# One-core decoder layer, routing stage reordered: turns of the second block between the first block's router products, residual products moved into later waits

## What is computed

```
x = x + mix @ w_out
h = rmsnorm(x, ln_ffn_g)
logits = h @ w_router + b_router            # 256 x 32
top_val, top_idx = top_k(logits, 4); probs = softmax(top_val)
# for each expert e, on the tokens that chose it:
a = clamped_swiglu(xb @ w_gate[e] + b_gate[e], xb @ w_up[e] + b_up[e])
y = a @ w_down[e] + b_down[e]
x = x + (sum over the chosen experts of prob * y)
out = rmsnorm(x, ln_final_g)
```

## Time and profile before

| | us |
|---|---|
| median of 3 runs | 1135.55 |
| lowest, highest | 1134.89, 1136.51 |
| the profiled execution | 1135.38 |
| its span | 1133.3 |
| TensorE busy | 1094.9 (97%) |
| VectorE busy | 315.9 (28%) |
| ScalarE busy | 205.5 (18%) |
| read from HBM | 437.69 MB, 387 GB/s over the span |

### The profile page before, as it was taken

How to read it: one execution, slowest core, us unless ns; L and a number is a source line. 1 busy time by engine, 2 the same in 40 slices (tenths; PEclk the granted TensorE clock), 3 DMA queues, 4 the chain that set the end, 5 groups by cost and what they waited for, 6 DMA issues and landing times.

```text
span 1133.3 us, 12456 instructions
## 1 busy us (share of the span) xinstructions
PE 1094.9 (97%) x5393; PEld 499.3 (44%) x5393; DVE 315.9 (28%) x684; ACT 205.5 (18%) x367; POOL 19.7 (2%) x27
## 2 busy tenths in 40 slices
PE   8999999999999999999999999999999999999997
PEld 6888888733343333333333333333333333333332
DVE  7566778421111111111211111111111111111121
ACT  6445547210000000001100000000000000000011
POOL 1000110000000000000000000000000000000000
PEclk9999999999999999999999999999999999999999
DMA  9754229999999999999999999999999999999996
GB/s 360 263 177 158 110 77 404 412 396 412 426 435 428 434 426 430 434 426 429 433 431 428 430 432 428 430 430 432 429 432 430 431 430 433 432 431 430 433 422 258
DMA packets 38439, 439.23 MB, mean 388 GB/s; under 512 B 3050, under 2 KB 4610, under 8 KB 19844
## 3 DMA queue, kind: packets, MB, share of 16 engines
q1 hardware_dynamic: 38100, 438.41, 92.2%
q10 hardware_dynamic: 304, 0.33, 0.1%
HBM read 437.69 MB, written 1.05 MB: 387 GB/s over the span
## 4 chain that ended last, share of the span: by engine, by line
PE 72%; DMA 25%; DVE 1%; issue 1%; ACT 0%; DVEq 0%; POOLq 0%; POOL 0%; ACTq 0%
PE ps L1153 42%; DMA pair<-in_w_up_dram 25%; PE ps L778 5%; PE ps L1177 5%; PE ps L1082 3%; PE ps L880 2%; PE ps L808 2%; PE ps L816 2%; PE ps L933 1%; PE ps L1130 1%; PE ps L935 1%; PE ps L934 1%; PE ps L1021 1%; PE ps L1023 1%; PE ps L1022 1%
## 5 line engine op out<-in xcount | busy, mean ns | idle before, releaser
L1153 PE MATMUL ps<-pair,o_t 128*64 128x512 f32 x3072 | 680.6, 595 | 23.2 <-DMA pair<-in_w_gate_dram 19.3
L1153 PEld LDWEIGHTS ps<-pair,o_t 128*64 128x64 f32 x3072 | 217.0, 137 | 442.6 <-issue 411.5
L1627 DVE TENSOR_SCALAR work<-ps 128x512 f32<-128x512 f32 x32 | 22.1, 692 | 494.9 <-PE ps L1153 494.9
L712 ACT ACTIVATE o_t<-ps 128x512 f32<-128x512 f32 x32 | 19.1, 597 | 297.9 <-PE ps L778 297.9
L1177 PE MATMUL ps<-attn,o_t 64*128 64x512 f32 x256 | 71.5, 639 | 0.0
L699 ACT ACTIVATE attn<-work 128x512 f32<-128x512 f32 x32 | 20.1, 629 | 261.2 <-DVE work L1627 261.2
L1082 PE MATMUL ps<-xs,work 128*64 128x512 f32 x256 | 61.0, 593 | 0.0
L778 PEld LDWEIGHTS ps<-cst,work 128*128 128x128 f32 (+1 forms) x294 | 35.8, 170 | 54.7 <-issue 52.1
L718 ACT ACTIVATE attn<-ps 128x512 f32<-128x512 f32 x31 | 18.5, 598 | 228.0 <-PE ps L1153 228.0
L778 PE MATMUL ps<-cst,work 128*128 128x128 f32 (+1 forms) x294 | 53.0, 296 | 1.0 <-DVE work L1444 0.6
L1633 DVE TENSOR_SCALAR a_rows<-ps 128x512 f32<-128x512 f32 x32 | 22.1, 692 | 103.1 <-PE ps L1153 103.1
(11 more groups left out here) (188 smaller groups left out, 845.6 us busy)
## 6 DMA issues: line engine op xcount, KB each, us to landing
pair<-in_w_gate_dram SPq DMA_DIRECT2D x27, 4096.0 KB, 38.6
pair<-in_w_up_dram SPq DMA_DIRECT2D x26, 4096.0 KB, 36.9
pair<-in_w_down_dram SPq DMA_DIRECT2D x25, 4096.0 KB, 38.3
pair<-in_w_up_dram SPq DMA_DIRECT2D x10, 2048.0 KB, 13.9
pair<-in_w_down_dram SPq DMA_DIRECT2D x9, 2048.0 KB, 14.9
pair<-in_w_gate_dram SPq DMA_DIRECT2D x8, 2048.0 KB, 13.3
wd<-in_w_in_dram SPq DMA_DIRECT2D x5, 2048.0 KB, 9.1
wu<-in_w_in_dram SPq DMA_DIRECT2D x4, 2048.0 KB, 10.8
```

The costliest lines, as they stand in the source:

```text
L1153: mm = pe.matmul(ps[SLOTS * h:SLOTS * h + SLOTS, bank, :], lhs[:, k, :], ring[(at + j) % RING][:, r, 512 * h:512 * h + 512], start=(k == 0 ...
```

## The change

Four edits, three of them on TensorE and one on ScalarE.

- The two calls `turn_residual(1, ...)`, which stood behind both calls of logits of block 0, now stand ahead of each of them. They get waits of their own, since they write banks that may still be read: (1,0) waits for VectorE's copy of (0,0), (1,1) for ScalarE's copy of (0,1).
- On ScalarE the turned copy of (1,0) changes places with the square of (1,1).
- The residual product of (0,0) moves from between the turns and the logits of block 1 to behind the first gather, where that of (0,1) stood. That of (0,1) is cut into two halves of 256 columns, which take the places of two pairs of fillers.
- The position product of block 0, which stood between the two calls of logits of block 1, now stands behind both.

```diff
@@ scalar
             square_residual(1, 0)
+            turned_residual(1, 0)
             square_residual(1, 1)
-            turned_residual(1, 0)
             turned_residual(1, 1)
@@ tensor
             def turn_residual(b, h):
                 pe.wait_ge(res_ready, 2 * b + h + 1)
+                if b and h:
+                    pe.wait_ge(ht_act, 1)
+                elif b:
+                    pe.wait_ge(ht_dve, 1)
@@
-            def residual_in(b, h, start=False):
+            def residual_in(b, h, cut=slice(0, 512), start=False):
-                pe.matmul(ps[:, Y + 2 * b + h, :], ident, xs[:, b, 512 * h:512 * h + 512], start=start, stop=False,
+                pe.matmul(ps[:, Y + 2 * b + h, cut], ident, xs[:, b, 512 * h:512 * h + 512][:, cut], start=start, stop=False,
                           skip_group_check=True)
@@
             pe.wait_ge(bias_lo_ready, 1)
+            turn_residual(1, 0)
             logits_of(0, 0)
+            turn_residual(1, 1)
             logits_of(0, 1)
-            turn_residual(1, 0)
-            turn_residual(1, 1)
-            residual_in(0, 0, start=True)
             logits_of(1, 0)
+            logits_of(1, 1)
             pe.wait_ge(chosen_ready, 1)
             pe.matmul(ps[:, DN, 0:E], tri_far, chosen[:, 0, :], start=True, stop=True).then_inc(pos0_done, 1)
-            logits_of(1, 1)
@@
             gather_block(0)
-            residual_in(0, 1, start=True)
+            residual_in(0, 0, start=True)
             pe.wait_ge(chosen_ready, 2)
             pe.matmul(ps[:, G, E:2 * E], tri_far, chosen[:, 1, :], start=False, stop=True).then_inc(pos_done, 1)
-            keep_busy(2)
+            residual_in(0, 1, cut=slice(0, 256), start=True)
@@
             mm.then_inc(count_done, 1)
-            keep_busy(2)
+            residual_in(0, 1, cut=slice(256, 512))
             turn_gathered(0)
```

## The result

The changed kernel is slower by a little: median 1137.51 us of 22 runs (1136.41 to 1138.34) against 1135.49 us of 22 runs of the kernel before (1134.88 to 1136.51), ratio 1.0017 with a 95% interval of 1.0011 to 1.0023. That is +2.0 us where I had forecast -0.2, and above the range's upper end of 1136.7. The profiled execution took 1136.60, span 1134.6; it lies 0.9 under the changed kernel's own median, so it probably shows a milder case of what the others have. Its routing stage begins 0.41 us earlier, counted from the start of the span (212.55 against 212.96), so places in this stage are compared after adding 0.41 to those of the changed kernel.

A forecast was written before the change was run, and what follows sets the result against it. Bound by the last expert's weights: a first product 0.15 to 0.37 us earlier gives back 0.2 of 0.99 us idle DMA; 1135.38 - 0.2 + 0.17 (median over profiled run) = 1135.35, forecast 1135.3 us, range 1134.3 to 1136.7.

The forecast's parts named there:

- What bounds the kernel: Whole kernel: the last expert's weights set the end; TensorE time counts only through 0.99 us of idle DMA at 225-228 us.
- Turns between logits: Routing stage, from 212.96 us: alternating block 1's turns with block 0's logits completes block 0's logits 1.02 us later.
- VectorE becomes what is late: Before the first gather: it waits for VectorE instead of TensorE's queue, starting at 218.42 instead of 218.79, gain 0.37 us.
- The residual product taken from there: At 215.69 us, ahead of block 1's logits: 0.96 us of TensorE work goes, those logits follow at once, issued by 217.38.
- The first gather to the second position product: Routing stage: gather plus one residual product still take 1.97 us, so the second position product starts at 220.4 to 220.5.
- The halves: Half residual products of 0.43 to 0.51 us in the fillers' places cost nothing; uncovered, each at most 0.2 us.
- The clock rival: Routing stage to first product: four fillers gone and two uncovered waits lower TensorE's clock, costing 3 to 6 us; chance 0.03.
- rivals: Transfers hide all, 1135.55, chance 0.2; block 0 late, 1135.9, 0.12; hole closes further, 1134.6, 0.05; clock lost, 1138-1142, 0.03.

The follow-up runs named there:

- the kernel without fillers: Kernel before without its five fillers behind the position product, the counts and the turned rows, down-bias products split over two experts: 1135.68 us, ratio 0.9999.
- the kernel with the turns alone: Changed kernel with the residual products and all fillers back in their old places: 1135.90 us, ratio 1.0003.
- without the second fall: Changed kernel with the down-bias products of block 1 moved from behind expert 3 to behind expert 4: 1136.43 us, ratio 1.0010.
- with four fillers: Changed kernel with four filler products between the logits of block 0 and those of block 1: 1135.96 us, ratio 1.0002.
- with both cures: Changed kernel with four filler products between the logits of blocks 0 and 1 and the down-bias products split over experts 3 and 4: 1136.19 us, ratio 1.0002.
- the kernel with the late product: Kernel before with five more fillers ahead of the turn of the gathered rows, delaying the first expert product: 1137.87 us, ratio 1.0015.

## Why the prediction was wrong, point by point

- **What bounds the kernel: right.** The end follows the weights. An added 1.06 us at the first product gave +1.0 at the end.
- **Turns between logits: right.** choose(0) was forecast at 215.94 and came at 215.45 + 0.41 = 215.86; its sum at 217.46, and it was 216.97 + 0.41 = 217.38.
- **VectorE becomes what is late: right.** The first gather was forecast at 218.42; it came at 217.84 + 0.41 = 218.25, with an idle stretch that VectorE ended. The gain of 0.37 us up to there was 0.54.
- **The residual product taken from there: this is the step that failed.** I wrote what TensorE no longer does and which queue profits, and gave the engine's clock as a constant. With the product gone TensorE ran nothing but narrow matmuls from 212.55 to 217.84; the clock fell, and the next 1.97 us of work took 3.56. +1.59 against the gain of 0.54 makes the first product 1.0 us later: 12.71 us behind the start of the stage (212.55 to 225.26) instead of 11.70.
- **The first gather to the second position product "is the same work in the new order": right as work, wrong as time.** For the same reason.
- **The halves: right.** The gather that follows the first waited for VectorE, not for them.
- **The clock rival had the right effect and the wrong cause.** It had 0.03. It tied the fall to four fillers gone and to waits of 0.1 and 0.3 us, and I set against it an idle stretch of 0.73 us at full clock. That argument was sound for what it spoke of, and the kernel without fillers bears it out. But it was the wrong question: TensorE was busy by the profile ahead of the fall (3.00 of 3.00 from 214 to 217 us). Here narrow matmuls filled the engine's busy time and the clock fell all the same. Its price, 3 to 6 us, was too high, since the clock came back before the first product: the first fall cost 1.59 us.
- **The Trainium skill** (page "TensorE: Matmul & The Clock Gate", section "HAM oscillation — how this bites in real kernels") ties the half rate to waits between bursts. Its example has waits for transfers of several microseconds, so it did not make the clock case the result of waits of 0.1 and 0.3 us, as the prediction has it. The only wait near the fall here is 0.19 us, it stands at full clock in the kernel with the turns alone, and ahead of it the engine's busy time was full and its work narrow. So the page pointed at the right danger and the trace at another way into it.
- **One sign was tied to the wrong step.** A first product later than 224.66 was to refute the step on VectorE. It came at 225.26, and the step on VectorE held; the delay arose behind the first gather.
- **Neither sum nor rivals had the second fall.** I had looked at 212 to 225 us alone. A shift of 1 us in everything behind it was taken to be a shift and no more. It brought a fall at the down-bias products, with a hole of 0.9 us of its own in the profiled run. Nor did I see why such a place is open to harm: early in the experts the weights in the ring wait for TensorE, and few loads are under way. The load issued at 344.17, when the product from 337.05 had freed its place, landed after 16.0 us, where the median over the span is 37 to 39. So a slow product there keeps the next load back and the DMA engines run short.
- **The range** was built from the spread of runs around one mechanism; the case that lay outside it had been left with 0.03.

By parts, against the kernel beside each: the changed kernel +2.0 us; without the second fall +1.1; with four fillers, which take the first fall away and most of the second with it, +0.2; with both cures +0.1.

What stays open: why the changed kernel had a low mean clock in each of its 22 runs and the kernel with only the residual products moved in about half; where the clock fell in the latter's slower runs; whether it is the width of the residual product that holds the clock or only the time that it takes; why a shift of 1 us brings the second fall; and the two runs above 1138 us of the changed kernel with split bias products. The mean clock of one run is too coarse to tell one fall from none in the routing stage.

## What to carry to other kernels

Before a wide matmul is moved out of a stretch of narrow ones, look at what is left between two wide ones: a product that looks like filler may be what holds TensorE's clock, and busy time will not say so. The test is cheap: put a few wide matmuls of no use in its place, and if the kernel gets faster with more work and the granted clock is back, it was the clock. And where an end is bound by transfers, a late start on TensorE comes back one for one through a ring that is full, and shifts what comes behind it into other stretches of thin work, so the granted clock is to be read over the whole span.

## What the runs showed of the hardware that I had not expected

- TensorE's granted clock fell to its lower level with the engine's busy time at 3.00 of 3.00 us ahead of it; the work there was 24 float32 instructions of 32 columns in a row and four more of position products, with transposes of 128 columns before them. The gather behind them took 1.98 instead of 1.08 us. A second place was the eight down-bias products, which use 32 of 128 rows; the product behind them took 8.41 instead of 7.09 us. In the kernel before the same products ran without a fall.
- Waits of 0.41 and 0.48 us between wide matmuls, without fillers, left the clock at 1.00.
- A fall of a few microseconds at 337 us, 360 us before TensorE first waits for weights, still cost 0.9 us of transfers in the changed kernel and, in the kernel with the late product, ran the transfers at 398 instead of 429 GB/s from 344 to 374 us (2.2 us; 2.7 by the landings). TensorE had seemed to have time to spare there, since it waits for no weights; but the loads were waiting for it.
